# A mixture-of-experts stage on one core: the up products of a pair ordered by expert, with a weight wait for each expert

## The reference

```python
MOE_TOP_K = 2; MOE_HIDDEN = 256; MOE_EXPERTS = 64; D_MODEL = 1024

def expert_block(args):
    xb, e = args
    hb = jax.nn.silu(xb @ w_gate[e]) * (xb @ w_up[e])
    return hb @ w_down[e]
```

## Time and profile before

| | us |
|---|---|
| median of 3 runs | 3430.31 |
| the profiled execution | 3427.95 |
| its span, first to last instruction | 3426.20 |
| first up product to the last pair's up products (starts) | 1319.84 to 1813.90 |

### The profile page before, as it was taken

The page is one execution under the profiler, slowest core; times in us unless marked ns, Lnnn a source line. Parts: engine busy times, 40 slices in busy tenths (PEclk is TensorE's granted clock), DMA queues, the critical chain, the costliest instruction groups (busy, mean ns, idle before and its releaser), DMA issues. The chain is left out here.

```text
span 3426.2 us, 36368 instructions
## 1 busy us (share of the span) xinstructions
PE 3106.4 (91%) x14832; PEld 2332.1 (68%) x14832; DVE 1400.2 (41%) x2156; ACT 931.2 (27%) x1480; POOL 190.0 (6%) x250
## 2 busy tenths in 40 slices
PE   7997778999898898877774999999999999999998
PEld 7886754667776585322222977888888788888887
DVE  3126846884444344111115647521215433333334
ACT  3532335663334220000003130121321332222221
POOL 0001022110000001111112000000000000000000
PEclk9998889999999999999996999999999999999999
DMA  3111000003220038999995131211112111111112
GB/s 99 47 49 5 9 14 1 1 1 117 73 82 13 25 149 344 419 420 420 415 413 212 38 78 59 66 46 50 37 56 105 50 62 50 50 50 46 47 50 80
DMA packets 141158, 372.17 MB, mean 109 GB/s; under 512 B 45952, under 2 KB 59904, under 8 KB 115008
## 3 DMA queue, kind: packets, MB, share of 16 engines
q1 hardware_dynamic: 130640, 349.06, 27.8%
q0 software_dynamic: 9216, 16.80, 1.3%
q10 hardware_dynamic: 1152, 4.19, 0.3%
HBM read 354.80 MB, written 32.83 MB: 113 GB/s over the span
## 5 line engine op out<-in xcount | busy, mean ns | idle before, releaser
L513 DVE TENSOR_TENSOR m_w_cut<-m_w_raw,m_w_cut 128x1024 fp32r<-128x1024 f32 (+1 forms) x153 | 162.9, 1065 | 792.5 <-ACT m_w_cut L509 791.8
L509 ACT ACTIVATE m_w_cut<-m_w_raw 128x1024 fp32r<-128x1024 f32 (+1 forms) x153 | 142.4, 930 | 1019.1 <-PE mlp_ps L622 521.3
L622 PE MATMUL mlp_ps<-mlp_high,m_w_cut 128*128 128x512 f32 x1024 | 315.7, 390 | 1.1 <-PEq L568 1.1
L622 PE MATMUL mlp_ps<-m_w_cut,mlp_hidden_high 128*128 128x512 f32 x1024 | 315.2, 389 | 0.0
L2839 PE MATMUL ffn_ps<-moe_wgu,moe_rowsT 128*64 128x512 f32 x1024 | 246.4, 637 | 52.1 <-issue 26.9
L622 PEld LDWEIGHTS mlp_ps<-mlp_high,m_w_cut 128*128 128x128 f32 x1024 | 191.8, 188 | 40.8 <-issue 1.3
L622 PEld LDWEIGHTS mlp_ps<-m_w_cut,mlp_hidden_high 128*128 128x128 f32 x1024 | 192.2, 188 | 39.9
L2839 PEld LDWEIGHTS ffn_ps<-moe_wgu,moe_rowsT 128*64 128x64 f32 x1024 | 79.7, 146 | 198.2 <-issue 170.1
L622 PE MATMUL mlp_ps<-mlp_low,m_w_cut 128*128 128x512 f32 x512 | 199.2, 389 | 0.0
L622 PE MATMUL mlp_ps<-m_w_cut,mlp_hidden_low 128*128 128x512 f32 x512 | 199.2, 389 | 0.0
L2875 DVE TENSOR_TENSOR moe_hid<-ffn_ps,moe_gated 128x256 f32<-128x256 f32 x32 | 13.6, 425 | 418.3 <-ACT moe_gated L2887 418.3
(11 more groups left out here) (570 smaller groups left out, 5921.2 us busy)
## 6 DMA issues: line engine op xcount, KB each, us to landing
moe_wgu<-in_moe_w_gate_dram SPq DMA_DIRECT2D x64, 1024.0 KB, 19.4
moe_wgu<-in_moe_w_up_dram SPq DMA_DIRECT2D x64, 1024.0 KB, 24.2
moe_wd<-in_moe_w_down_dram SPq DMA_DIRECT2D x64, 1024.0 KB, 25.6
m_w_raw<-in_w_ff_dram SPq DMA_DIRECT2D x68, 512.0 KB, 3.5
m_w_raw<-in_w_in_dram SPq DMA_DIRECT2D x48, 256.0 KB, 2.8
mix_w_raw<-in_w_in_dram SPq DMA_DIRECT2D x40, 256.0 KB, 2.6
m_w_raw<-in_w_in_dram SPq DMA_DIRECT2D x20, 512.0 KB, 3.5
x_w_raw<-in_x_w_kv_dram SPq DMA_DIRECT2D x16, 512.0 KB, 3.5
```

What stands on the lines that cost most here:

```text
L509: nc.scalar.activation(part(s, 0).bitcast(F32R), raw(s), ACT.Copy).then_inc(high_ready, 1)
L513: nc.vector.tensor_tensor(part(s, 1).bitcast(F32R), raw(s), part(s, 0), ALU.subtract).then_inc(low_ready, 1)
L622: ins = nc.tensor.matmul(ps[:, place, :r.shape[-1]], l, r, start=(k == 0 and sw is high and wh == 0), stop=(k == job.nk - 1 and sw is low))
```

## The change

It does three things.

1. `up` runs the expert loop outside and the k loop inside: 16 instruction pairs for expert 0, then 16 for expert 1. The last matmul of each expert adds one to `up_done`, which so counts to two a pair; every wait on it is doubled to match.
2. Each expert of a place has its own semaphore for its gate and up weights (`gu_in[w][h]`, 32 a fill). TensorE waits for expert 0's ahead of expert 0's products and for expert 1's between the two. SyncE waits for the release of each expert's part by itself: expert 0's two transfers are issued when the products of expert 0 three pairs back are done, expert 1's when those of expert 1 are.
3. The three more held semaphores are made up for: the seven of RowsNorm are no longer held, and a `c.recycle(0)` stands ahead of the projection `x_kv_up`.

```diff
-            c.hold_sem(f"x_rows_{n}") for n in (
+            c.sem(f"x_rows_{n}") for n in (
...
+        c.recycle(0)
         project(c, "x_kv_up", stream, kv_jobs, banks=MEM // P, following=q_jobs,
...
-            [sem(f"{name}_gate_up_in{b}") for b in range(small)], [sem(f"{name}_down_in{b}") for b in range(small)])
+            [[sem(f"{name}_gate_up_in{b}_{h}") for h in range(parts)] for b in range(small)], [sem(f"{name}_down_in{b}") for b in range(small)])
...
-    before[0]()
     for h in range(parts):
+        before[0](h)
         for i in range(2):
             load_half(sp, a, weights, w, parts, expert, h, i)
     before[1]()
...
-    sp.dma_start(wgu[:, w * parts + h, i].rearrange("p k n -> p (k n)"), src).then_inc(gu_in[w], 16)
+    sp.dma_start(wgu[:, w * parts + h, i].rearrange("p k n -> p (k n)"), src).then_inc(gu_in[w][h], 16)
...
-            (lambda: wait_for(sp, self.up_done, n - self.slots + 1),
+            (lambda h: wait_for(sp, self.up_done, self.parts * (n - self.slots) + h + 1),
...
         pe.wait_ge(self.rowsT_ready, n + 1)
-        w, i, each = b % self.slots, b % self.small, 32 * self.parts
-        pe.wait_ge(self.gu_in[w], each * self.filled(b, use) + each)
+        w, i = b % self.slots, b % self.small
         wait_for(pe, self.hid_ready, n - self.small + 1)
-        for k in range(KD):
-            for h in range(self.parts):
-                r = slice(h * P // self.parts, (h + 1) * P // self.parts)
+        for h in range(self.parts):
+            pe.wait_ge(self.gu_in[w][h], 32 * self.filled(b, use) + 32)
+            r = slice(h * P // self.parts, (h + 1) * P // self.parts)
+            for k in range(KD):
                 ins = self.nc.tensor.matmul(self.ps_h[r, i].rearrange("p (i n) -> p i n", i=2), self.rowsT[:, i, k, r],
                                             self.wgu[:, w * self.parts + h, :, k], start=(k == 0), stop=(k == KD - 1))
-        ins.then_inc(self.up_done, 1)
+            ins.then_inc(self.up_done, 1)
...
-        wait_for(dve, self.up_done, n - self.small + 1)
+        wait_for(dve, self.up_done, self.parts * (n - self.small + 1))
...
-        act.wait_ge(self.up_done, n + 1)
+        act.wait_ge(self.up_done, self.parts * (n + 1))
```

More of the change, by code:

```diff
@@ L2705, in expert_weights, with load_expert_weights @@
             sbuf(ctx, c.nc, f"{name}_wd", [P, small * parts, EH // P, D]),
-            [sem(f"{name}_gate_up_in{b}") for b in range(small)], [sem(f"{name}_down_in{b}") for b in range(small)])
-def load_expert_weights(sp, a, weights, w, parts, expert, before=(lambda: None, lambda: None)):
-    before[0]()
+            [[sem(f"{name}_gate_up_in{b}_{h}") for h in range(parts)] for b in range(small)], [sem(f"{name}_down_in{b}") for b in range(small)])
+def load_expert_weights(sp, a, weights, w, parts, expert, before=(lambda h: None, lambda: None)):
     for h in range(parts):
+        before[0](h)
         for i in range(2):
@@ L3024, in moe_first @@
             st = first.steps
-            one = (weights[0][:, 0:1], weights[1][:, 0:1], [c.sem("over_gate_up_in")], [c.sem("over_down_in")])
+            one = (weights[0][:, 0:1], weights[1][:, 0:1], [[c.sem("over_gate_up_in")]], [c.sem("over_down_in")])
             st = ExpertSteps(c, run, "over", a, xn, y, gain, slot_tok, slot_row, 1, 1, 1, 1, one,
```

## The result

| | before | after |
|---|---|---|
| median, us | 3430.31 (3 runs) | 3516.80 (3 runs, 3514.06 to 3525.50) |
| span of the profiled execution | 3426.2 | 3512.3 |
| first to last start of an up group | 494.06 | 586.89 |

The ratio is 1.0267, 95% interval 1.0251 to 1.0283. The same kernel in five more runs gave 3525.11, ratio 1.0280 (1.0260 to 1.0299), a loss of 98 us against 3427.21 of the kernel before in the same session.

The account below looks back on a forecast made before the run. The weights bound most of the expert stage at 16.80 us a pair; after the change TensorE would, at 19.67 us. Stage +117.1 and last group +4.3 give +121.4 us, so 3552 us, range 3530 to 3595.

Parts of the forecast that it names:

- the wait between the experts is met: Up products: TensorE's new wait for expert 1's weights is already met when reached and costs nothing.
- the clock fell in the wait: Last up group before the change: takes 8.78 us because the clock had fallen in a wait of 2.06 us.
- near 320: Expert stage's transfers: 6.3 MB of weights in 19.67 us a pair, 320 GB/s, of 420 shown.
- part 1: Up products' new order: most overlap of the two experts is lost, group 13.04 us, 5.95 more.
- I take three as it is shown: Up group: TensorE passes three waiting instructions, so two slots are shared and the group has 30 slots, 13.04 us.
- the 0.80 that I gave to 29 to 32 slots: Chance of the forecast as worked out: up group of 29 to 32 slots, 3538 to 3579 us.
- 19.67 forecast: Expert stage: TensorE's time a pair, 13.72 + 5.95 us, over the weights' 16.80 us.
- the forecast's 121.4: Whole kernel: us added, +117.1 from first to last up group and +4.3 for the last group.
- A: Up group: engine picks from the whole queue, overlap stays, group near 7.5 us, kernel 3428 us; chance 0.10.
- its threshold: Expert stage: a longer TensorE pair is free until it passes 16.80 us, 3.08 us or 7 slots more.
- B: Up group: each load of 0.137 us adds to its slot, group 18.1 us, +285, 3715 us; chance 0.04.
- C: Up group: 7 to 13 slots more, from a look-ahead of 6 to 18 instructions, 3440 to 3535 us; chance 0.06.

Follow-up runs that it names:

- order_only: Kernel before with only the up products' order changed, all eight k-slices of expert 0 then of expert 1, one wait and release: 3520.92 us, ratio 1.0281.
- waits_only: Changed kernel with its waits, releases and semaphores, but up products alternating again and both waits ahead of them: 3427.91 us, ratio 1.0006 against the kernel before.
- after_again: The changed kernel run and profiled once more, nothing altered: 3525.11 us (5 runs), ratio 1.0280 against the kernel before.

## Why the prediction was right in kind and wrong in size

**Right.** TensorE bounds the whole stage, 18.85 us a pair from the first pair to the last. The order is the cause (order_only), the waits, releases and semaphores are nothing (waits_only), the wait between the experts is met, no weight is late, loads hide behind matmuls (a slot stays 0.43 us with a load of 0.14 us in it), and all that stands between two groups stays. SyncE waits for the up group throughout (57 waits in 32 pairs, two releases a pair). The last group has neither the wait ahead of it nor the low clock now: granted 0.58 from 1813.90 to 1818 before, 1.00 after, and it takes 12.24 us. That the clock fell in the wait, as the prediction says, was not shown: before, it was granted 1.00 from 1811.84 to 1813.90, the wait itself, and 1.00 from 1461.12 to 1468, behind a wait of 2.55 us. One sign was off beside the sizes: the DMA engines move 360 GB/s and not near 320: the weights alone are 6.29 MB in 18.85 us, 334 GB/s, and the prediction left out the rows and results that are moved beside them, 2.45 of the 36.23 MB from 1400 to 1500.

**The step that failed** is in part 1: "I take three as it is shown", which gave 30 slots and 13.04 us. A group has 28 slots. In the last group's timeline and windows this can be counted. The timeline's weight loads come one in a slot; then, 5.15 us into the group, three, two and two:

```profile
1899.95 0.14 PEld L2840 LDWEIGHTS ffn_ps<-moe_wgu,moe_rowsT 128*64 128x64 f32 x1 [0.29 <-issue]
1900.38 0.19 PEld L2840 LDWEIGHTS ffn_ps<-moe_wgu,moe_rowsT 128*64 128x64 f32 x3 [0.29 <-issue]
1900.81 0.19 PEld L2840 LDWEIGHTS ffn_ps<-moe_wgu,moe_rowsT 128*64 128x64 f32 x2 [0.24 <-issue]
1901.24 0.19 PEld L2840 LDWEIGHTS ffn_ps<-moe_wgu,moe_rowsT 128*64 128x64 f32 x2 [0.23 <-issue]
1901.73 0.14 PEld L2840 LDWEIGHTS ffn_ps<-moe_wgu,moe_rowsT 128*64 128x64 f32 x1 [0.29 <-issue]
```

```profile
1899.90:1900.30 0.40, 0.40 (x2) 0.14 (x1) 0.00 (x0) 0.00 (x0) 0.00 (x0) 1.00 0.11 41
1900.33:1900.73 0.40, 0.40 (x3) 0.19 (x3) 0.00 (x0) 0.00 (x0) 0.00 (x0) 1.00 0.00 0
```

Two matmuls touch a stretch of 0.40 us (one ends, one starts), and in the next three do: expert 0's thirteenth matmul starts at 1900.38, twelve slots of 0.429 after the first, and expert 1's first beside it. At that moment a matmul, a load, a matmul, a load and a matmul of expert 0 stand unstarted ahead of it: five are passed, and slots 13 to 16 are shared. 12 + 4 + 12 = 28 slots; 27 x 0.429 = 11.6 us to the last start, 11.64 measured in this group and 11.70 in most. I was two slots off. One is the look-ahead, five (or six) instead of three. The other is my own counting: the three that I had read from the alternating stream is a depth at which both halves are always fed, and an idle half takes a load and its matmul within 0.02 us, a slot earlier than I let it. With room for three the theory above has 29 slots, 12.6 us, and with six 28, where I had 29. What the trace of before showed was a lower bound of the look-ahead, since there nothing needed more, and I took the bound for the value; the 0.80 that I gave to 29 to 32 slots should have been spread to fewer.

**The sizes.** 29 intervals are 0.77 us shorter than the 19.67 forecast (18.90, mean of the 29 from 1329.37 on), 22.3 us. The last interval is 17.73, 1.9 shorter: 0.8 by the group, 1.1 since no rows are left to turn in it. The last group is 0.8 shorter than 13.04. That makes 25 of the 25.1 us between the forecast's 121.4 and the 96.3 measured. The remaining 10 us down to 86 are the profiled execution's, from long before the stage, where it had the higher clock (0.86 against 0.72 from 460 to 520); in after_again the two spans lie 97.1 apart. The medians say the same: 86 us with three runs of the changed kernel, 98 with five. So some 24 of the 35 us that the forecast was off are the mis-sized group, and they alone put the time below the range (3525.11 in the five runs).

**The rivals.** A (all overlap stays) fell, and its threshold with it: 15.94, not 16.80 us. B (loads exposed) fell, at 0.43 us a slot. C had the time (3440 to 3535) and the slots (7 to 13 more; 12 came), but asked for a look-ahead of 6 to 18, where five is enough; with room for six, which the runs leave open, its condition would just hold. Three of expert 1's matmuls start ahead of expert 0's last in the changed kernel's group: 0, 1 and 2 slots behind expert 0's thirteenth.

## What to carry to other kernels

In this kernel, products that use different columns of the array ran side by side only where the order brought them within about five instructions of each other: alternate them, in runs of at most two f32 products (last start at 6.55 us in runs of two, 8.38 in runs of four), and look at a group's span over its count of matmuls, not at the busy share, which rose here from 80 to 92% while the kernel took 2.7% longer. A depth that a trace shows in use is a lower bound; before you build on it, ask what the same trace would look like if it were deeper. And where a stage starts with a stock of work ahead, the pace that is free is the stage's length over its intervals, not the spacing at its end.

## What the runs showed that I had not expected

The look-ahead between the halves of the columns comes out as five instructions (six would fit too) from last starts of 6.55 to 11.70 us, while the sequencer runs 34 ahead: the 34 didn't help expert 1, whose first matmul starts 5.15 us into the group, with expert 0's thirteenth. The DMA share reads 0.94 to 0.95 at 359 to 363 GB/s after, and 1.02 at 420 before, with landings three times as quick; a share near 1 was no sign here that the transfers are the bound, and what told it were the waits. With 1 MB transfers split in halves along k, the rate was 377 to 413 GB/s instead of 413 to 420. The granted clock between 460 and 520 us differs by 0.12 between two executions of one program, and their stages begin 12 us apart.
